# A modulation vector on GpSimd: whole-unit multiply and halving sums, or 512-column products summed one by one

## The chip, the cores and the metric

The kernel runs on one core of a Trainium2 chip. The metric is the device time of one execution in microseconds; the profile gives one execution in detail, on that core. Engines are named as the profile names them: PE (TensorE matmul), PEld (its weight load), DVE (VectorE), ACT (ScalarE), POOL (GpSimd) and SP (the queue that issues the weight loads).

## The reference

Two blocks run one after the other over 256 tokens of width 1024, all in float32. The first is a two-layer mixer (gated recurrence, latent attention, memory attention, each layer ending in a layer norm), the second has attention, pooling and a layer of 16384 experts. The part that the change touches is the modulation of the second block, which depends on `c` alone and on nothing that the first block computes:

```python
mod = jnp.einsum('bd,de->be', jax.nn.silu(c), w_ada[l]) + b_ada[l]      # (1, 1024) x (1024, 6144)
sh1, sc1, g1, sh2, sc2, g2 = jnp.split(mod[:, None, :], N_MOD, axis=-1)
h = rmsnorm(x, norm1_g[l]) * (1.0 + sc1) + sh1
```

## The kernel before

The order of all work is written out by hand as a text of tasks, `LAYER` for each of the two layers and `BLOCK2` for the second block; every engine walks the same text and takes its part of each task. The weights arrive in units of 2 MB (1024 rows by 512 columns, laid out as 128 partitions by 8 chunks of 512) in a ring of three slots. The load of unit n is issued by SP when PE has counted unit n - 3 as done.

Twelve of the tasks are called `AD`, six in each layer: each makes 512 of the 6144 numbers of the modulation vector. GpSimd works on the unit where it lies. The chunk index c and the partition p together are the row of the weight, and `silu_c` (a view into tile `lbt`, 128 x 8) holds silu(c) in the same layout, so what is wanted is the sum over c of `w[:, c, :] * silu_c[:, c]`, a 128 x 512 tile called `part` (half of `mod_part`, the two halves in turn), which PE then sums over the partitions with four small matmuls (line 761) and DVE adds to the bias (line 1329). GpSimd does it in four instructions, each of which waits for the one before by `pool_step`: line 510 multiplies all 4096 columns, with `silu_c` broadcast along the 512 columns of a chunk; line 511 adds the upper four chunks to the lower four (2048 columns), line 512 the upper two of these to the lower two (1024 columns), line 513 the last two into `part` (512 columns). PE waits on `mod_partial` before line 761, and counts the unit as done after it.

The places of the `AD` tasks in `LAYER` that the steps below speak of:

- the first of a layer stands in the text after `F1 Da01 Da02 Db01 L00 A0`; but GpSimd starts as soon as its unit has landed, while PE still runs F1 (line 570, 64 matmuls) and DVE the rotations of UP (lines 1440, 1442 and 1443). DVE then takes F1 from PSUM (line 1359), does `Da01`, `Da02` and `Db01` (two instructions each: lines 1385 and 1389 twice, then 1396 and 1397), and PE's matmuls of level 1 (line 726) wait for `Db01`.
- the second of a layer runs beside Q1 (PE line 570).
- the fifth and sixth close the layer: `O2 L18 H10 AD H11 AD H12 O3 O1 LN`. H10, H11 and H12 are short matmuls on PE (lines 742 to 744 and 751), O3 and O1 are output products (line 608).

DVE instructions that matter in what follows read two operands from SBUF: line 1350 (`sm` times a broadcast of `stat`), 1385 and 1389 (differences of `b`), 1396 and 1397 (`big` times `kT` or `qT`), 1442 and 1443. Lines 1359, 1411, 1455 and 1476 read one operand from PSUM. The scores of a head, line 622 on PE, are taken from PSUM by line 1455.

After the two layers the second block runs; from about 970 us on, its experts fetch 8 KB rows by indirect DMA, with DVE, ACT and PE behind the DMA.

Of the kernel before, what the change touches and what calls it, by code (L numbers as in the profile page):

```python
# [14 lines left out]
P = 128  # L15
# [3 lines left out]
DC = D_MODEL // P  # L19
# [11 lines left out]
COLS = 512  # L31
# [137 lines left out]
def part_starts():  # L169

    return {tile * PICKS + first * TOPK: n + 1 for n, (tile, first, last) in enumerate(EXPERT_PARTS)}
# [48 lines left out]
def build(nc, d, out):  # L220
# [10 lines left out]
    with ExitStack() as ctx:  # L231
# [58 lines left out]
        silu_c = lbt[:, 4, :]  # L290
# [41 lines left out]
        def sem(name):  # L332
            if name not in made:
                made[name] = ctx.enter_context(nc.semaphore(name))
            return made[name]
# [19 lines left out]
        def bank_filled(eng, key):  # L355
            eng.wait_ge(sem("bank_filled"), BANK[key] + 1)
# [18 lines left out]
        def ring_loads(n):  # L375

            units = range(n % RING, n + 1, RING)
            return 16 * sum(3 if STREAM[k][1] == "UP" else 1 for k in units)

        def unit_done(eng, l, name):  # L380
            eng.wait_ge(sem("unit_done"), UNIT[l, name] + 1)

        def steps(eng, own):


            seen = {}

            def step(ins, name=None, value=None, behind=0):
                name = name or own
                seen[name] = value or seen.get(name, 0) + 1  # L390
                ins.then_inc(sem(name), 1)
                eng.wait_ge(sem(name), seen[name] - behind)
            return step
# [100 lines left out]
        @block.gpsimd  # L494
        def _(pool):
            g = nc.gpsimd
            do = steps(pool, "pool_step")

            pool.wait_ge(sem("silu_c"), 1)
            for l in range(DEPTH + 1):  # L500
                for task in TASKS[l]:
                    if task[:2] == "AD":
                        j, n = int(task[2:]), UNIT[l, task]
                        pool.wait_ge(sem(f"ring_load{n % RING}"), ring_loads(n))
                        if j >= 2:
                            key = (l, (f"AD{j - 2}",)) if (l, (f"AD{j - 2}",)) in BANK else (l - 1, (f"AD{j - 2}",))
                            bank_filled(pool, key)
                        w = ring[:, n % RING, :].rearrange("p (c n) -> p c n", c=DC)
                        part = mod_part[:, j % 2, :]
                        do(g.tensor_tensor(w, w, silu_c.unsqueeze(2).to_broadcast([P, DC, COLS]), ALU.mult))  # L510
                        do(g.tensor_tensor(w[:, 0:4, :], w[:, 0:4, :], w[:, 4:8, :], ALU.add))  # L511
                        do(g.tensor_tensor(w[:, 0:2, :], w[:, 0:2, :], w[:, 2:4, :], ALU.add))
                        do(g.tensor_tensor(part, w[:, 0, :], w[:, 1, :], ALU.add), "mod_partial")

            pool.wait_ge(sem("uT_ready"), 1)
            pool.wait_ge(sem("b2_load"), 16 * N_B2)
            do(g.tensor_copy(pool_sum, uT))
            for w in range(4):
                for k in range(w + 1):
                    n = 2 ** k  # L520
                    spare = mixed[:, w, :]
                    do(g.tensor_copy(spare, pool_sum[:, w, :]))
                    do(g.tensor_tensor(pool_sum[:, w, n:T], spare[:, n:T], spare[:, 0:T - n], ALU.add))
            do(g.tensor_tensor(mixed, pool_sum, inv_count.rearrange("p (a t) -> p a t", a=4), ALU.mult))
            do(g.tensor_tensor(mixed, mixed, uT, ALU.subtract), "pool_mixed")


            starts = part_starts()
            for n in range(ROWS):
                t, j, k = n // PICKS, n % PICKS, n % N_SLOTS  # L530
                if n in starts:
                    pool.wait_ge(sem("experts"), starts[n])
                if n >= N_SLOTS:
                    pool.wait_ge(sem("rows_used"), n - N_SLOTS + 1)
                elif n in freed_with:
                    if freed_with[n][0] == "K":
                        unit_done(pool, B2, freed_with[n])
                    else:
                        bank_filled(pool, (B2, ("E", 7)))
                pool.indirect_dma_start(row_slot[k], None, d["peer_uv_2"],  # L540
                                        bass.IndirectOffsetOnAxis(ap=expert[:, t, j:j + 1], axis=0))\
                    .then_inc(sem(f"row_load{k}"), 16)
# [696 lines left out]
        def _(dve):  # L1239
# [112 lines left out]
            for l in range(DEPTH):  # L1352
                for task in TASKS[l]:
# [25 lines left out]
                    elif task[:2] == "Da":  # L1379
                        g, m = int(task[2]), int(task[3])  # L1380
                        if m >= 3:

                            bank_filled(dve, (l, ("L", g, m - 3, 1)))
                        b0, b1, w0, w1, _, _, mid = level_views(g, m)
                        do(v.tensor_tensor(w0, mid, b0, ALU.subtract))
                        if m == 8:
# [3 lines left out]
                    elif task[:2] == "Db":  # L1390
                        g, m = int(task[2]), int(task[3])
                        after(dve, "lvl_exp", l, 8 * g + m - 1)
                        _, _, w0, w1, k0, q1, _ = level_views(g, m)
                        if m == 1:
                            after(dve, "q_ready", l, g)
# [366 lines left out]
```

## Time and profile before

| | us |
|---|---|
| median of three runs | 1699.2 (1698.88 to 1701.31) |
| the profiled execution, its own time | 1703.25 |
| its span | 1701.4 |
| PE busy | 1433.9 (84%) |
| DVE busy | 895.8 (53%) |
| POOL busy | 451.8 (27%) |
| POOL line 510, 12 instructions | 84.6, mean 7.048 |
| POOL line 511, 12 instructions | 56.7, mean 4.729 |
| POOL line 512, 12 instructions | 29.8, mean 2.487 |
| POOL line 513, 12 instructions | 17.8, mean 1.487 |

The span is the time from the first to the last instruction of the profiled execution; its own time is 1.85 us longer and lies 4.05 us above the median of the three runs. Busy time is a sum over instructions, not a share of what sets the end. The twelve modulation units keep GpSimd busy for 188.9 us together, all of it between 102 and 800 us of the span.

### The profile page before, as it was taken

The numbers are of one execution on the slowest core, as the hardware profiler recorded it, in microseconds if no ns is written. First come the engines' busy times: TensorE is split into PE (matmuls) and PEld (weight loads), VectorE is DVE, ScalarE is ACT, GpSimd is POOL, SyncE is SP. The second block draws the span as 40 slices with busy tenths as digits, with TensorE's granted clock in tenths as the row PEclk, the third lists the DMA queues.
The fourth block names the chain that finished last, engine by engine and source line by source line (L and its number), as shares of the span: only waits on it lengthen the run. The fifth ranks groups of instructions, "written<-read, shape, count | busy, mean of one in ns | idle before, by whom it ended". The sixth has DMA issues, their size and how long they took to land.

```text
span 1701.4 us, 14497 instructions
## 1 busy us (share of the span) xinstructions
PE 1433.9 (84%) x4979; PEld 891.3 (52%) x4979; DVE 895.8 (53%) x1689; ACT 425.0 (25%) x1035; POOL 451.8 (27%) x331
## 2 busy tenths in 40 slices
PE   7989898799998898799797988978767888777875
PEld 6768576565767757574374477423322333333332
DVE  2276834544047944643404257785798555444443
ACT  2322232311142214220212223322223222222222
POOL 0033330042003630007004002534333433333330
PEclk9989898999999889899898899989988999899998
DMA  7323442225342435125522137999999999999993
GB/s 261 130 100 104 148 159 84 99 100 219 124 148 80 168 108 189 50 99 192 177 99 99 50 109 299 422 422 421 422 421 421 421 422 421 422 422 421 421 422 134
DMA packets 97460, 401.06 MB, mean 236 GB/s; under 512 B 5765, under 2 KB 9706, under 8 KB 64618
## 3 DMA queue, kind: packets, MB, share of 16 engines
q0 software_dynamic: 36864, 268.45, 38.1%
q1 hardware_dynamic: 60522, 131.68, 21.7%
q8 instruction: 40, 0.66, 0.2%
q14 instruction: 34, 0.28, 0.0%
HBM read 399.06 MB, written 1.05 MB: 235 GB/s over the span
## 4 chain that ended last, share of the span: by engine, by line
PE 53%; DMA 22%; DVE 11%; issue 6%; ACT 6%; POOL 1%; ACTq 0%; SPq 0%; DVEq 0%; POOLq 0%
PE pj L570 21%; DMA ring<-in_peer_uv,vM 9%; PE bank L927 8%; PE pj L608 7%; PE pj L583 5%; PE bank L726 3%; DMA kM<-in_peer_uv,vM 3%; DMA hv<-in_peer_uv,vM 3%; DMA yT<-in_peer_uv,vM 3%; PE bank L638 2%; DMA more_rows<-in_peer_uv,vM 2%; DMA b<-in_peer_uv,vM 1%; PE bank L552 1%; DMA qM<-in_peer_uv,vM 1%; PE bank L622 1%
## 5 line engine op out<-in xcount | busy, mean ns | idle before, releaser
L570 PE MATMUL pj<-xT,ring 128*128 128x256 f32 (+1 forms) x1664 | 373.8, 387 | 2.3 <-ACTq L976 2.3
L570 PEld LDWEIGHTS pj<-xT,ring 128*128 128x128 f32 (+1 forms) x1664 | 318.8, 193 | 55.1 <-issue 5.8
L510 POOL TENSOR_TENSOR ring<-ring,lbt 128x4096 f32<-128x4096 f32 x12 | 84.6, 7048 | 607.6 <-issue 475.4
L540 POOL DMA_INDIRECT ring<-in_peer_uv,vM x102 | 95.7, 939 | 168.3 <-PE bank L927 139.7
L608 PE MATMUL pj<-ring,yT 128*128 128x512 f32 x320 | 138.9, 593 | 0.9 <-ACTq L1180 0.5
L927 PE MATMUL bank<-ring,far_pair 128*128 128x512 f32 x208 | 103.4, 650 | 31.0 <-ACT far_pair L1215 31.0
L1207 ACT ACTIVATE rope<-vM 128x4 f32<-128x4 f32 x64 | 13.1, 205 | 450.7 <-DVE big L1685 450.6
L927 PE MATMUL bank<-ring,causal 128*128 128x512 f32 x200 | 97.6, 639 | 21.5 <-ACT causal L1215 20.3
L608 PEld LDWEIGHTS pj<-ring,yT 128*128 128x128 f32 x320 | 60.3, 190 | 75.5 <-issue 73.7
L726 PE MATMUL bank<-big 128*128 128x128 f32 x480 | 79.5, 332 | 15.4 <-DVE big L1397 10.4
L927 PEld LDWEIGHTS bank<-ring,far_pair 128*128 128x128 f32 x208 | 42.5, 209 | 91.1 <-issue 51.6
L726 PEld LDWEIGHTS bank<-big 128*128 128x128 f32 x480 | 75.5, 242 | 24.7 <-DVE big L1397 11.2
L1685 DVE SCALAR_TENSOR_TENSOR pair<-ring,pj 128x1024 f32<-128x1024 f32 x51 | 62.2, 1220 | 48.6 <-DMA ring<-in_peer_uv,vM 44.5
L1685 DVE SCALAR_TENSOR_TENSOR big<-ring,pj 128x1024 f32<-128x1024 f32 x51 | 62.2, 1220 | 46.8 <-DMA ring<-in_peer_uv,vM 46.8
L927 PEld LDWEIGHTS bank<-ring,causal 128*128 128x128 f32 x200 | 40.1, 204 | 77.8 <-issue 50.4
L1045 ACT ACTIVATE big<-big 128x1024 f32<-128x1024 f32 x32 | 33.8, 1058 | 128.2 <-DVE big L1389 124.3
L583 PE MATMUL pj<-ring,xT 128*128 128x512 f32 x128 | 57.6, 609 | 0.0
L1411 DVE COPY_PREDICATED pair<-level_mask,bank 128x512 f32<-128x512 uint8 x56 | 40.8, 729 | 30.9 <-PE bank L726 29.3
L511 POOL TENSOR_TENSOR ring<-ring 128x2048 f32<-128x2048 f32 x12 | 56.7, 4729 | 0.9
L982 ACT ACTIVATE sm<-sm,stat 128x256 f32<-128x256 f32 x64 | 32.5, 508 | 94.3 <-DVE stat L1460 69.9
L1209 ACT ACTIVATE rope<-rope,rstd 128x1 f32<-128x1 f32 x256 | 54.4, 282 | 2.1
L540 POOL DMA_INDIRECT more_rows<-in_peer_uv,vM x18 | 18.0, 998 | 117.9 <-DVE vM L1596 86.5
(341 smaller groups left out, 2273.1 us busy)
## 6 DMA issues: line engine op xcount, KB each, us to landing
ring<-in_w_in SPq DMA_DIRECT2D x26, 2048.0 KB, 7.9
ring<-in_w_ada SPq DMA_DIRECT2D x12, 2048.0 KB, 8.0
ring<-in_w_out SPq DMA_DIRECT2D x10, 2048.0 KB, 7.8
ring<-in_peer_wq SPq DMA_DIRECT2D x4, 2048.0 KB, 8.0
ring<-in_w_mem_k SPq DMA_DIRECT2D x2, 2048.0 KB, 11.9
ring<-in_w_mem_v SPq DMA_DIRECT2D x2, 2048.0 KB, 9.3
ring<-in_w_in SPq DMA_DIRECT2D x2, 1664.0 KB, 9.6
ring<-in_peer_uv,vM POOLq DMA_INDIRECT x102, 24.8
```

The source lines that it names most:

```text
L510: do(g.tensor_tensor(w, w, silu_c.unsqueeze(2).to_broadcast([P, DC, COLS]), ALU.mult))
L511: do(g.tensor_tensor(w[:, 0:4, :], w[:, 0:4, :], w[:, 4:8, :], ALU.add))
L540: pool.indirect_dma_start(row_slot[k], None, d["peer_uv_2"], bass.IndirectOffsetOnAxis(ap=expert[:, t, j:j + 1], axis=0))\
L570: ins = nc.tensor.matmul(pj[s][0:n, 2 * m:2 * m + T], w[:, c, m:m + n], act[:, c, :], start=(c == 0), stop=(c == DC - 1))
L583: ins = nc.tensor.matmul(pj[s][:, t * COLS:(t + 1) * COLS], act[:, c, t * P:(t + 1) * P], w[:, c, :], start=(c == 0), stop=(c == DC - 1))
L608: ins = nc.tensor.matmul(pj[t][:, n * 512:(n + 1) * 512], yT[:, 4 * j + c, t * P:(t + 1) * P], w[:, c, n * 512:(n + 1) * 512], start=(firs ...
L638: ins = nc.tensor.matmul(bank_of(key)[rows, 0:T], v[s], pT[:, i % 2, s, :], start=(s == 0), stop=(s == TT - 1))
L726: ins = nc.tensor.matmul(B[:, n * P:(n + 1) * P], k, q, start=True, stop=True)
L927: ins = nc.tensor.matmul(bank[2 * t + half][:, :], diag[n % N_DIAG], row_slot[n % N_SLOTS][:, c0:c0 + COLS], start=(j == 0), stop=(j == PI ...
L1209: a.activation(weights_of[:, n0 + k:n0 + k + 1], acts[:, n0 + k:n0 + k + 1], ACT.Copy, scale=gate[:, t, j + k:j + k + 1]).then_inc(sem("ro ...
L1411: do(v.copy_predicated(dst, level_mask[:, m - 1:m, :].to_broadcast([P, 4, P]), B), *bank_free(key))
L1685: v.scalar_tensor_tensor(out=junk[n % 2], in0=row_slot[k][:, 0:D_MODEL], scalar=1.0, in1=pj[BIG[l, f"K{2 + t}"][0]][:, :], op0=ALU.mult, o ...
```

## The change

On GpSimd the four instructions of a unit become fifteen, all over 512 columns. The first multiplies chunk 0 by a scalar per partition, `silu_c[:, 0:1]`, straight into `part`. Then for each of the seven other chunks one instruction multiplies the chunk in place by its scalar, and one adds it to `part`. Each still waits for the one before. The last addition gives `mod_partial`. Nothing else in the kernel differs.

```diff
-                        do(g.tensor_tensor(w, w, silu_c.unsqueeze(2).to_broadcast([P, DC, COLS]), ALU.mult))
-                        do(g.tensor_tensor(w[:, 0:4, :], w[:, 0:4, :], w[:, 4:8, :], ALU.add))
-                        do(g.tensor_tensor(w[:, 0:2, :], w[:, 0:2, :], w[:, 2:4, :], ALU.add))
-                        do(g.tensor_tensor(part, w[:, 0, :], w[:, 1, :], ALU.add), "mod_partial")
+                        do(g.tensor_scalar(part, w[:, 0, :], silu_c[:, 0:1], None, ALU.mult))
+                        for c in range(1, DC):
+                            do(g.tensor_scalar(w[:, c, :], w[:, c, :], silu_c[:, c:c + 1], None, ALU.mult))
+                            do(g.tensor_tensor(part, part, w[:, c, :], ALU.add), "mod_partial" if c == DC - 1 else None)
```

The order of instructions is the same as before on PE, DVE, ACT and SP. On POOL, at the twelfth unit (the last `AD` of the second layer, after which its next work is the copy of line 517 in the second block), it was:

```order
L510 TENSOR_TENSOR ring<-ring,lbt 128x4096 [waits bank_filled,ring_load2,mod_partial]
L511 TENSOR_TENSOR ring<-ring 128x2048 [waits pool_step]
L512 TENSOR_TENSOR ring<-ring 128x1024 [waits pool_step]
L513 TENSOR_TENSOR mod_part<-ring 128x512 [waits pool_step]
L517 COPY kT<-kT 128x1024 [waits b2_load,uT_ready,mod_partial]
```

The same unit begins now with these rows, of which the second and third come seven times:

```order
L510 TENSOR_SCALAR mod_part<-ring,lbt 128x512 [waits bank_filled,ring_load2,mod_partial]
L512 TENSOR_SCALAR ring<-ring,lbt 128x512 [waits pool_step]
L513 TENSOR_TENSOR mod_part<-mod_part,ring 128x512 [waits pool_step]
L512 TENSOR_SCALAR ring<-ring,lbt 128x512 [waits pool_step]
L513 TENSOR_TENSOR mod_part<-mod_part,ring 128x512 [waits pool_step]
```

Four rows in a chain have become fifteen in a chain, with the same waits at the head; the wait for the unit's bank now stands ahead of the first write to `mod_part`, where it stood before too. On PE the end of the same unit is awaited here, between H11 (line 751) and H12 (the second row of line 751), as before:

```order
L751 MATMUL bank<-sq,ones_mean 128x512 [waits ho_sq,bank_free2]
L761 MATMUL bank<-ones_mean,mod_part 128x1 [waits mod_partial,bank_free3]
L761 MATMUL bank<-ones_mean,mod_part 128x1 x3
L751 MATMUL bank<-sq,ones_mean 128x512 [waits bank_filled,ho_sq,bank_free0]
L608 MATMUL pj<-ring,yT 128x512 [waits ring_load0,y_att]
```

No row of PE has moved; what changes there is only when `mod_partial` comes.

## Rows read from the trace of the kernel before

**Rows 1.** The page: busy time, share of the span and instructions of each engine

```profile
PE 1433.9 (84%) x4979; PEld 891.3 (52%) x4979; DVE 895.8 (53%) x1689; ACT 425.0 (25%) x1035; POOL 451.8 (27%) x331
```

**Rows 2.** Chain that ended last, 764 to 812 us: start, us, what

```profile
775.80 5.67 DMA ring<-in_w_ada
781.47 3.08 issue
784.55 7.03 POOL ring L510
...
791.64 4.52 POOL ring L511
...
796.23 2.35 POOL ring L512
...
798.65 1.27 POOL mod_part L513
...
800.06 1.04 PE bank L761 x8
```

**Rows 3.** Timeline of PE, 384 to 400 us, layer 1: start, us, instruction, idle before

```profile
393.17 1.02 PE L761 MATMUL bank<-ones_mean,mod_part 128*128 128x1 f32 x8 [0.98 <-POOL mod_part L513]
394.50 1.10 PE L751 MATMUL bank<-sq,ones_mean 128*128 128x512 f32 x2 [0.30 <-ACT sq L1104]
```

**Rows 4.** Timeline of POOL, 911 to 915 us: copies with one input

```profile
911.97 1.03 POOL L517 COPY kT<-kT 128x1024 f32<-128x1024 f32 x1 [112.05 <-ACTq L1152]
913.06 0.40 POOL L522 COPY b<-kT 128x256 f32<-128x256 f32 x1
```

**Rows 5.** Waits: who waited for whom, us in total, times, longest

```profile
PE bank L726 <- DVE big L1397: 10.4, 2, 5.6
```

**Rows 6.** Timeline of DVE, 511 to 531 us, first unit of layer 2

```profile
511.63 6.81 DVE L1442 TENSOR_TENSOR qM<-qM,rope 32x512 f32<-32x512 f32 x1
518.47 4.88 DVE L1443 TENSOR_TENSOR qM<-qM,sm 32x512 f32<-32x512 f32 x1
523.39 1.23 DVE L1359 TENSOR_SCALAR b<-pj 128x1024 f32<-128x1024 f32 x1
524.76 1.36 DVE L1385 TENSOR_TENSOR big<-b 128x512 f32<-128x512 f32 x1
526.16 1.63 DVE L1389 TENSOR_TENSOR big<-b 128x512 f32<-128x512 f32 x1
...
530.01 0.69 DVE L1397 TENSOR_TENSOR big<-big,qT 128x512 f32<-128x512 f32 x1
```

**Rows 7.** Timeline of POOL, 510 to 530 us, the same unit

```profile
510.88 7.02 POOL L510 TENSOR_TENSOR ring<-ring,lbt 128x4096 f32<-128x4096 f32 x1 [117.85 <-issue]
517.97 4.84 POOL L511 TENSOR_TENSOR ring<-ring 128x2048 f32<-128x2048 f32 x1
...
525.65 1.59 POOL L513 TENSOR_TENSOR mod_part<-ring 128x512 f32<-128x512 f32 x1
```

**Rows 8.** Timeline of PE, 505 to 535 us, the same stretch

```profile
507.00 15.55 PE L570 MATMUL pj<-xT,ring 128*128 128x256 f32 x64
...
530.76 3.54 PE L726 MATMUL bank<-big 128*128 128x128 f32 x16 [5.56 <-DVE big L1397]
```

**Rows 9.** Timeline of POOL, first unit of layer 1

```profile
102.72 7.24 POOL L510 TENSOR_TENSOR ring<-ring,lbt 128x4096 f32<-128x4096 f32 x1 [102.27 <-DMA ring<-in_w_ada]
```

**Rows 10.** Timeline of DVE, the same unit

```profile
116.49 1.37 DVE L1385 TENSOR_TENSOR big<-b 128x512 f32<-128x512 f32 x1
```

**Rows 11.** Timeline of PE, the same unit

```profile
122.49 2.72 PE L726 MATMUL bank<-big 128*128 128x128 f32 x11 [4.83 <-DVE big L1397]
```

**Rows 12.** Timelines of PE, then of DVE, second unit of layer 2

```profile
574.81 1.03 PE L622 MATMUL bank<-kM,qM 96*128 96x256 f32 x4
...
576.76 0.69 DVE L1455 SCALAR_TENSOR_TENSOR sm<-bank,causal 128x512 f32<-128x512 f32 x1 [0.21 <-DVE pair L1411]
...
557.64 7.28 DVE L1350 TENSOR_TENSOR sm<-sm,stat 128x512 f32<-128x512 f32 x1
```

## The prediction

> **What bounds the kernel now.** I read the page first. PE is busy 84% of the span, DVE 53%, POOL 27% [rows 1], and that 27% counts the expert fetches of the second half too. So GpSimd's throughput binds nothing. Its modulation work can matter in two ways only: PE waits for a unit's result, or DVE, sharing something with it, becomes late while PE waits for DVE. The second view, the chain that ended last, names the one place where the first way holds: the twelfth unit. Its load is issued at 775.80, GpSimd starts at 784.55, and its four instructions lie end to end in the chain until PE's line 761 at 800.06, behind which line 751 and the output products follow without another wait [rows 2]. The sixth unit, the same place one layer earlier, is nearly as tight: PE idles 0.98 us until GpSimd's line 513 ends, starts line 761 at 393.17 and line 751 at 394.50, for which ACT had been ready at about the same time [rows 3]. All other units are finished long before PE wants them.
>
> For the second way I looked at the timelines of DVE and POOL side by side. DVE's line 1442, with two inputs in SBUF, takes 6.81 us at 511.63, where line 1397, of the same kind, takes 0.69 us at 530.01 [rows 6]. Line 510 on POOL runs from 510.88 to 517.90 [rows 7], and the DVE instruction ends at 518.44, 0.54 us behind it. The same holds at 526.16: line 1389 ends at 527.79, 0.55 us behind the end of line 513 (525.65 + 1.59 = 527.24). So a DVE instruction with two SBUF inputs stands still until the POOL instruction under way ends. The price on the other side is small: line 513 takes 1.59 us here and 1.27 us in the chain of the twelfth unit [rows 7, 2], so a POOL instruction that finds DVE inside is 0.33 us longer, once. Is PE late through this? The view of waits has one line that says so: line 726 waits for DVE's line 1397 twice, 10.4 us in all [rows 5]; these are the first units of the two layers [rows 8, 11]. In the other units PE is in a long product while DVE stands still.
>
> **The cost of a unit.** Undisturbed, before: 784.55 to 799.92, so 15.37 us, gaps of 0.07 us between instructions included [rows 2]. After: 7 additions over 512 columns at 1.27 us, the line 513 of the chain, make 8.89; 14 gaps make 0.98; and 8 products by a scalar over 512 columns, of which the trace has none. From below: a copy, one input and one output, takes 1.03 us over 1024 columns and 0.40 over 256 [rows 4], a line that gives 0.61 at 512. From above: line 510, which reads a second operand for each element, if only by broadcast. Take from the additions what an instruction costs beside its elements: 4.52, 2.35 and 1.27 us over 2048, 1024 and 512 columns [rows 2] leave 0.18 us at zero columns; then 7.03 us over 4096 columns is 1.67 ns a column, and 512 of them are 1.03 us. I take 0.80, about the middle, a little nearer the copy: the product reads one stream like the copy, but fetches a scalar and multiplies. The unit is then 6.40 + 8.89 + 0.98 = 16.3 us, **0.9 us more** than before; with the copy's price 14.75 (0.6 less), with the broadcast's 18.1 (2.7 more). What was won by touching less data in wide sums is little, since both forms multiply 4096 columns and add 3584.
>
> By the Trainium skill (GPSIMD Engine Reference, section 3.1) a tight loop on GpSimd took 769 ns for 512 elements, which as a price of the product would make the unit 16.0 us and the sum about 1 us smaller.
>
> **Where it is paid.**
> - Twelfth unit: on the path whole, +0.9. Its start is set by its load (775.80), which waits for an output product and not for GpSimd; the eleventh unit leaves 3.08 us of nothing before it [rows 2] and can end up to 3.1 us later before it holds this one up.
> - Sixth unit: PE waits for it already, and line 751 follows 1.33 us behind the start of line 761 [rows 3], +0.9. A gain here would be worth nothing, since ACT's `sq` released line 751 too.
> - First unit of layer 2. DVE no longer stands still for 6.8 and 4.9 us at 511.63, and can start line 1359 when PE's F1 is in (507.00 + 15.55) instead of at 523.39 [rows 8, 6]: its first line 1385 starts at 523.9, 0.8 us earlier. But GpSimd is not through by then: of its 16.3 us, 12.4 are done (13.0 less two delays of 0.33), 3.9 are left, nearly four pieces of 1.09, and each now meets one DVE instruction, so they last 5.2 us, to 529.1. DVE does one instruction for each, so four, is free at 529.65, does the last two at 0.73 each and ends at 531.1, where before it was 530.70: +0.4.
> - First unit of layer 1, in the same way: GpSimd starts at 102.72, line 1385 on DVE at 116.49 [rows 9, 10]. 13.4 us are done by then, 2.8 left, three pieces, to 120.3 with three delays; DVE is free at 120.85 and ends its last three at 123.0; before, PE's line 726 was released at 122.44 [rows 11]: +0.6.
> - Second unit of layer 2: the scores are in PSUM about 1.58 us behind the start of line 622, at 576.39, the lag that the same pair has in layer 1; DVE took them at 576.76, because contended instructions had made it late [rows 12]. With pieces it is in time: -0.4.
> - The other seven: nothing. DVE stands still inside products of PE's of some 15 us (that of 507.00 is one [rows 8]) and has caught up at their end, since the one line of the waits that has PE behind a contended DVE instruction counts two cases [rows 5]; with pieces it is never later. If that cover were thinner, DVE's relief would be a gain (below), not a loss.
> - PE's, ACT's, DVE's and SP's instructions and all loads stay. The eleven more instructions a unit cost issue time only in the gaps, counted above.
>
> Sum: 0.9 + 0.9 + 0.4 + 0.6 - 0.4 = **+2.4 us**, on an execution of 1703.25 whose span is 1701.4. Its own time lies 4.05 above the median of the runs, 1699.2; put on that median, the change gives **1701.6 us**. It is 0.14%; a measurement of this kernel tells about 0.2%, 3.4 us, from no change.
>
> **The rivals.**
> 1. *The scalar product is as cheap as a copy*, 0.61 us. The unit is 0.6 us shorter: twelfth -0.6, sixth 0, first of layer 2 -0.4 (2.35 us left at 523.9, two pieces), first of layer 1 -0.6, second -0.4: -2.0, or 1697.2. For it: one stream in, one out. Against it: the scalar. Within the 0.2% all the same. The Trainium skill says of this (GPSIMD Engine Reference, section 4.1) that operations with one input run at roughly line rate on GpSimd; the copies agree, and whether a product with a scalar operand does no row shows.
> 2. *The scalar product costs what the broadcast product does*, 1.03 us, and the change ends slower. Place: the sixth and twelfth units, on PE's path. The unit is 2.7 us longer: +5.4 there; first of layer 2 +1.9 (5.7 us left, five pieces), first of layer 1 +2.1, second -0.4: +9.0, or 1708.2. It passes 3.4 us from about 0.84 us a product on. For it: on this engine every element passes through a program, and 15 short instructions pay 15 launches. Against it: half the operands.
> 3. *DVE's relief is worth more than I let it be.* In the first and second units of layer 2, DVE's lines 1442, 1443 and 1350 take 6.81, 4.88 and 7.28 us in place of 0.69 [rows 6, 12], 16.9 us of standing still. If PE truly ran behind DVE there, these would come back, at 1682.3 if nothing is lost elsewhere. Against it: in the same stretch PE's F1 ends at 522.55 only and the next product at about 575, so at most 0.8 and 0.4 us are free [rows 8, 12]. The rule behind it is in the Trainium skill (SBUF — State Buffer, Who interferes with whom): GpSimd and a DVE instruction with two SBUF inputs exclude each other for the whole instruction, so shorter instructions would mean shorter waits. The trace agrees on the wait [rows 6, 7]; it is PE's products that make it nearly worthless.
>
> **How the numbers follow.** The forecast, with the product at 0.68 to 0.88 us, holds 0.45 (sums of -0.5 to +4.7); rival 1 0.25, rival 2 0.25, rival 3 0.05. Slower by over 0.2% is rival 2 and the third of the forecast above 0.84 us: 0.40. Faster by over 0.2% is rival 3 and 0.03 of rival 1, if a measurement adds its own: 0.08. The rest is 0.52. The range takes in rivals 1 and 2 and 0.3 to 0.7 us of scatter at either end: 1696.5 to 1708.5; left out are rival 3 and prices above the broadcast's.
>
> **What would show it.** On POOL, products (lines 510 and 512) with a duration of 0.80 us and additions at 1.27, or 1.6 where DVE meets them; a twelfth unit of 16.3 us from its load to PE's line 761, which then starts about 16.4 us behind it. On DVE no instruction of 512 columns above about 2 us before 800 us, so less busy time by some tens of microseconds. PE's line 726 released by DVE later by about half a microsecond in the first units. The prediction is wrong if the twelfth unit is shorter than before or longer than 17.5 us, or if PE's start of the output products at the end of either layer comes earlier by several microseconds, which would be rival 3.

## The result and the profile after

| | us |
|---|---|
| changed kernel, median of four runs | 1726.23 (1720.21 to 1727.65) |
| kernel before, beside it | 1699.12 (1698.88 to 1701.31) |
| ratio | 1.0136, interval 1.0108 to 1.0165 |
| profiled execution of the changed kernel | 1727.65, its span 1725.9 |

The change makes the kernel slower by 1.4%, outside the range that was given. The medians lie 27.1 us apart, and the span of the profiled execution grew by 24.5 us. The page's first part and the groups of the three changed lines (us busy, mean ns of one, idle before):

```profile
PE 1439.8 (83%) x4979; PEld 893.8 (52%) x4979; DVE 832.1 (48%) x1689; ACT 424.9 (25%) x1035; POOL 529.2 (31%) x463
...
L510 POOL TENSOR_SCALAR mod_part<-ring,lbt 128x512 f32<-128x512 f32 x12 | 18.8, 1567 | 540.4 <-issue 417.0
...
L512 POOL TENSOR_SCALAR ring<-ring,lbt 128x512 f32<-128x512 f32 x84 | 138.6, 1650 | 8.2
...
L513 POOL TENSOR_TENSOR mod_part<-mod_part,ring 128x512 f32<-128x512 f32 x84 | 109.1, 1299 | 7.0
```

DVE is busy 63.7 us less than in [rows 1]. POOL is busy 77.4 us more, and the cause stands in the first two groups: a product by a scalar takes 1.56 us or more, where the forecast had 0.80. The additions cost what was expected. POOL's timeline through the end of layer 2 shows the price of one unit and what it does to the next:

```profile
776.80 1.61 POOL L510 TENSOR_SCALAR mod_part<-ring,lbt 128x512 f32<-128x512 f32 x1 [116.12 <-issue]
778.50 1.56 POOL L512 TENSOR_SCALAR ring<-ring,lbt 128x512 f32<-128x512 f32 x1
780.14 1.26 POOL L513 TENSOR_TENSOR mod_part<-mod_part,ring 128x512 f32<-128x512 f32 x1
...
798.22 1.26 POOL L513 TENSOR_TENSOR mod_part<-mod_part,ring 128x512 f32<-128x512 f32 x1
799.58 1.56 POOL L510 TENSOR_SCALAR mod_part<-ring,lbt 128x512 f32<-128x512 f32 x1
...
816.28 1.88 POOL L512 TENSOR_SCALAR ring<-ring,lbt 128x512 f32<-128x512 f32 x1
...
821.25 1.26 POOL L513 TENSOR_TENSOR mod_part<-mod_part,ring 128x512 f32<-128x512 f32 x1
```

The eleventh unit runs from 776.80 to 799.48, 22.7 us instead of 15.4. It passes the 3.08 us of nothing that lay ahead of the twelfth [rows 2], so the twelfth starts on its heels, at 799.58, and takes 22.9 us itself. PE meets both delays at once. Its timeline at the end of layer 1 and of layer 2 in the changed kernel, then at the end of layer 2 in the kernel before:

```profile
385.89 0.95 PE L761 MATMUL bank<-ones_mean,mod_part 128*128 128x1 f32 x8
...
388.56 1.02 PE L751 MATMUL bank<-sq,ones_mean 128*128 128x512 f32 x2
402.98 1.83 PE L761 MATMUL bank<-ones_mean,mod_part 128*128 128x1 f32 x8 [13.40 <-POOL mod_part L513]
405.12 2.04 PE L751 MATMUL bank<-sq,ones_mean 128*128 128x512 f32 x2 [0.30 <-PE bank L761]
...
822.66 1.83 PE L761 MATMUL bank<-ones_mean,mod_part 128*128 128x1 f32 x8 [13.41 <-POOL mod_part L513]
824.79 2.05 PE L751 MATMUL bank<-sq,ones_mean 128*128 128x512 f32 x2 [0.30 <-PE bank L761]
```

```profile
800.06 1.02 PE L761 MATMUL bank<-ones_mean,mod_part 128*128 128x1 f32 x8 [1.89 <-POOL mod_part L513]
801.39 1.10 PE L751 MATMUL bank<-sq,ones_mean 128*128 128x512 f32 x2 [0.30 <-PE bank L761]
```

And its line in the waits (us in total, times, longest), now and before:

```profile
PE bank L761 <- POOL mod_part L513: 26.8, 2, 13.4
```

```profile
PE bank L761 <- POOL mod_part L513: 2.9, 2, 1.9
```

PE waits 23.9 us more for GpSimd. It also comes back slower: lines 761 and 751 take 1.83 and 2.04 us where they took 1.02 and 1.10 [rows 3]. The stretches show the granted clock there; first the changed kernel, then the one before (us, busy time of PE, PEld, DVE, ACT and POOL with instructions, granted clock, DMA share, GB/s):

```profile
385.00:400.00 15.00, 4.28 (x32) 3.40 (x30) 6.03 (x9) 2.51 (x4) 14.09 (x11) 0.83 0.86 332
400.00:410.00 10.00, 6.72 (x16) 4.01 (x17) 1.43 (x3) 1.32 (x2) 2.75 (x2) 0.58 0.34 114
```

```profile
400.00:410.00 10.00, 10.00 (x24) 4.37 (x23) 4.18 (x6) 0.91 (x2) 0.00 (x0) 1.00 0.61 229
```

After 13.4 us in which PE did nothing the mean grant over ten microseconds is 0.58, near the lower of the two levels (1.2 of 2.4 GHz), where before it was 1.00. That costs 1.75 us on lines 761 and 751 at the end of each layer, and 0.75 and 0.83 us on the 64 output products behind them (27.63 us before, 28.38 and 28.46 now).

In time order the 24.5 us are: -2.6 up to the fifth unit's line 761 (388.50 before, 385.89 now), +13.7 from there to the eleventh unit's (405.98 to 419.66 us long), +13.4 from there to the end. Longer waits and late return together make 29.0 us, more than the whole. The -2.6 is within the scatter: four executions further down whose early units are wide reach that line between 384.11 and 388.96 us. Another 1.9 us come back in PE's other work behind it, of which 1.3 lie in a stretch of layer 2 where the grant was 0.93 instead of 0.92.

DVE's long standing still is gone, as expected, and hardly matters for the time. In the first unit of layer 1, DVE, then POOL and PE:

```profile
102.56 0.81 DVE L1442 TENSOR_TENSOR qM<-qM,rope 32x512 f32<-32x512 f32 x1
103.41 0.68 DVE L1443 TENSOR_TENSOR qM<-qM,sm 32x512 f32<-32x512 f32 x1
...
116.49 1.06 DVE L1389 TENSOR_TENSOR big<-b 128x512 f32<-128x512 f32 x1
117.58 0.69 DVE L1385 TENSOR_TENSOR big<-b 128x512 f32<-128x512 f32 x1
118.31 1.64 DVE L1389 TENSOR_TENSOR big<-b 128x512 f32<-128x512 f32 x1
```

```profile
116.00 1.88 POOL L512 TENSOR_SCALAR ring<-ring,lbt 128x512 f32<-128x512 f32 x1
117.97 1.43 POOL L513 TENSOR_TENSOR mod_part<-mod_part,ring 128x512 f32<-128x512 f32 x1
```

```profile
121.83 3.62 PE L726 MATMUL bank<-big 128*128 128x128 f32 x16 [5.65 <-DVE big L1397]
```

No DVE instruction on two SBUF inputs lasts over 1.7 us there, yet PE waits for it 5.65 us where it waited 4.83 [rows 11].

These rows also show that the two forms on POOL don't hold DVE up alike. The DVE instruction at 118.31 ends at 119.95, 0.55 us behind the addition that it met (117.97 + 1.43). The one at 116.49 ends at 117.55, 0.33 us before the product by a scalar that it met (116.00 + 1.88), and has lost only 0.37 us. In the whole changed kernel it is the same: of DVE's lines 1385, 1389, 1396 and 1397, the fourteen that began beside an addition ended 0.54 to 0.56 us behind it, and the twelve that began in the first 0.7 us of a product by a scalar ended 0.33 to 0.34 us before its end.

### The profile page after: what moved, and what is told of

The parts are those of the page before. It is cut to its first block, busy times and chain, and to the rows that moved or that the text cites. A ratio compares the mean times of both kernels' runs of the same rounds, so it can differ in the third digit from the quotient of the medians.

```text
span 1725.9 us, 14629 instructions
## 1 busy us (share of the span) xinstructions
PE 1439.8 (83%) x4979; PEld 893.8 (52%) x4979; DVE 832.1 (48%) x1689; ACT 424.9 (25%) x1035; POOL 529.2 (31%) x463
## 4 chain that ended last, share of the span: by engine, by line
PE 30%; DMA 22%; issue 11%; DVE 7%; ACT 3%; POOL 3%; ACTq 0%; DVEq 0%; POOLq 0%
PE pj L570 10%; DMA ring<-in_peer_uv,vM 8%; PE bank L927 7%; PE pj L608 5%; DMA yT<-in_peer_uv,vM 4%; DMA kM<-in_peer_uv,vM 3%; DMA hv<-in_peer_uv,vM 3%; PE pj L583 2%; DMA b<-in_peer_uv,vM 1%; DMA qvE<-in_peer_uv,vM 1%; POOL ring L512 1%; DMA qM<-in_peer_uv,vM 1%; POOL mod_part L513 1%; PE pj L676 1%; PE bank L726 1%
## 5 line engine op out<-in xcount | busy, mean ns | idle before, releaser
L570 PE MATMUL pj<-xT,ring 128*128 128x256 f32 (+1 forms) x1664 | 369.9, 384 | 2.3 <-ACTq L976 2.3
L510 POOL TENSOR_SCALAR mod_part<-ring,lbt 128x512 f32<-128x512 f32 x12 | 18.8, 1567 | 540.4 <-issue 417.0
L512 POOL TENSOR_SCALAR ring<-ring,lbt 128x512 f32<-128x512 f32 x84 | 138.6, 1650 | 8.2
L513 POOL TENSOR_TENSOR mod_part<-mod_part,ring 128x512 f32<-128x512 f32 x84 | 109.1, 1299 | 7.0
L726 PE MATMUL bank<-big 128*128 128x128 f32 x480 | 79.8, 332 | 16.3 <-DVE big L1397 11.2
L1455 DVE SCALAR_TENSOR_TENSOR sm<-bank,causal 128x512 f32<-128x512 f32 x16 | 11.1, 692 | 102.7 <-PE bank L552 80.6
```

What stands on the lines that cost most here:

```text
L510: do(g.tensor_scalar(part, w[:, 0, :], silu_c[:, 0:1], None, ALU.mult))
L512: do(g.tensor_scalar(w[:, c, :], w[:, c, :], silu_c[:, c:c + 1], None, ALU.mult))
L513: do(g.tensor_tensor(part, part, w[:, c, :], ALU.add), "mod_partial" if c == DC - 1 else None)
L570: ins = nc.tensor.matmul(pj[s][0:n, 2 * m:2 * m + T], w[:, c, m:m + n], act[:, c, :], start=(c == 0), stop=(c == DC - 1))
L726: ins = nc.tensor.matmul(B[:, n * P:(n + 1) * P], k, q, start=True, stop=True)
```

## The experiments

Three questions were put. Does the loss lie in the two units that close each layer, and there alone? What in the product makes it dear? And is DVE's relief worth something where nothing hides it? In kernels that hold both forms, all lines behind 510 stand six higher. The kernel before, measured beside each, has run medians of 1699 to 1706 us. Its granted clock over an execution lies between 0.911 and 0.927, and its span goes with it by about -0.84 us for each 0.001 (94 executions, correlation -0.65); differences of a few microseconds are read from stretches of the trace for that reason.

**The old form in the last two units of each layer**

```diff
+if j % 6 < 4:      # pieces, as in the change
+else:              # the four wide instructions
```

> The last two units of each layer in the old four instructions, the first four in the fifteen pieces. Theory A (the product by a scalar costs 1.56 us, and this is paid only where PE waits for the last unit of a layer): PE's wait before line 761 falls from 13.4 us back to about 1 to 2 in both layers, and the time is that of before or 1 to 3 us below it, 1696 to 1699. Rival B (the pieces cost time everywhere, by taking turns with DVE eight times more often): four of six units still pay, about two thirds of the 25 us, 1712 to 1716.

Measured: 1700.01 us (1695.86 to 1706.84), ratio 0.9985 [0.9963, 1.0008]. PE waits 2.5 us for GpSimd. With eight of twelve units in the new form nothing measurable is lost or won.

**The new form in the last two units alone**

```diff
+if j % 6 >= 4:     # pieces; else wide
```

> The reverse: only the last two units of each layer in pieces. Theory A: the whole loss is here, PE's waits of about 13 us are back, 1723 to 1728. Rival B: a third of the loss, 1705 to 1709.

Measured: 1723.3 us (1720.79 to 1726.44), ratio 1.0125 [1.0081, 1.0169], wait 26.8 us. Repeated:

> The kernel with the last two units of each layer in scalar pieces, once more. As it ran the first time: about 20 us above before.

1724.83 us, 1.0144 [1.0102, 1.0185], wait 26.8 again. Four units of twelve carry the loss.

**The new form in the very last unit of each layer**

```diff
+if j % 6 == 5:     # pieces; else wide
```

> Only the last unit of each layer in pieces, so that the fifth ends early and does not hold up the sixth. Theory A: the unit is 22.6 us in place of 15.4, PE waits 7.2 us longer twice, so 14.5 us, and up to 3 more if PE comes back at a lower clock: 1713 to 1717. If instead the whole loss came from the last unit alone, it would stay at 1724 or more. Rival B: a sixth of the loss, 1703.

> The kernel with only the last unit of each layer in scalar pieces, once more. If the first result was a matter of the clock, it now lies 14 to 19 us above before and below the run with the last two units, with granted clocks alike in the two. If a long wait costs more than its length, it again lies at 23 and not below the other.

The wait did what was expected: 17.3 us (8.55 and 8.73), 9.5 less than with both units, which is the part that the fifth and eleventh hand on. The time did not: 1726.2 us, 1.0142 [1.01, 1.0184], and in the repetition 1726.58, 1.0145 [1.0107, 1.0182], where at most 1717 was expected. Here are three stretches that run the same program, from layer 2's first product on `xT` (line 576) to the second unit's line 767: this kernel twice, then the one with both units new.

```profile
450.31:596.40 146.09, 133.75 (x580) 106.41 (x580) 81.37 (x90) 36.02 (x52) 34.67 (x9) 0.90 0.34 119
```

```profile
452.20:598.12 145.92, 133.75 (x581) 106.38 (x581) 80.96 (x90) 36.03 (x52) 34.28 (x9) 0.90 0.34 119
```

```profile
451.44:593.25 141.81, 128.11 (x581) 103.45 (x581) 80.63 (x89) 36.10 (x52) 33.44 (x9) 0.93 0.35 122
```

The last kernel's repetition has 141.73 us at 0.93. The same instructions take 4.2 us longer at a grant of 0.90, with PE 5.6 us busier. From the last line 767 to the first expert fetch, 748 PE instructions in each, it is 220.84 and 220.98 us at 0.89 against 216.87 and 216.40 at 0.91; from that fetch to the end all four lie between 683.8 and 684.4. So about 8 us of the gap goes with the clock and not with the wait for GpSimd. Up to the fifth unit's line 767 another 2.9 us lie between the two kernels on average, although PE waits for GpSimd in neither. Whether the grant follows from how layer 1 ended, and how, is open; the kernel before lies between, 143.48 us at 0.92.

**Products with a broadcast scalar, in pieces**

```diff
-g.tensor_scalar(w[:, c, :], w[:, c, :], silu_c[:, c:c + 1], None, ALU.mult)
+g.tensor_tensor(w[:, c, :], w[:, c, :], silu_c[:, c:c + 1].to_broadcast([P, COLS]), ALU.mult)
```

> The same fifteen pieces, but each product as a product of two tensors with the scalar broadcast along 512 columns, as in the old line 510. Theory A (it is the scalar form that is dear): 1.03 us a piece in place of 1.56, a unit of 18.1 us, the fifth no longer holds up the sixth, +2.7 us a layer: 1702 to 1706. Rival C (any short instruction is dear, by its launch): the pieces stay near 1.5 us, and the time near 1724.

Measured: 1712.94 us (1709.83 to 1715.19), ratio 1.0068 [1.0048, 1.0088]; wait 9.8 us.

```profile
L512 POOL TENSOR_TENSOR ring<-ring,lbt 128x512 f32<-128x512 f32 x84 | 93.5, 1114 | 6.6
...
L510 POOL TENSOR_TENSOR mod_part<-ring,lbt 128x512 f32<-128x512 f32 x12 | 12.8, 1069 | 573.0 <-issue 444.5 <-DMA ring<-in_w_ada 128.0 <-POOL mod_part L513 0.5
```

The form that reads a second operand for every element costs 1.07 us, the one that holds a scalar 1.57. This one edit gives back half of the loss. It was expected at 1702 to 1706 and missed by 7 us. Two things were not in that sum. The wait of 4.71 us at the end of layer 1 already makes lines 761 and 751 come back at 1.41 and 2.04 us. And in the first units PE waits for DVE 13.9 us in all, where it waited 10.4 before and 11.2 with scalar products: beside a broadcast product DVE stands still to 0.55 us behind its end, as beside an addition.

**The scalar products, then the old wide sums**

```diff
+for c in range(DC): g.tensor_scalar(w[:, c, :], ..., ALU.mult)
+# then the three wide additions of the kernel before
```

> Eight products by a scalar over 512 columns in place of line 510, then the old wide additions. Theory A: 8 x 1.56 + gaps + 8.1 = 21.3 us a unit, 5.9 more than before; the fifth unit ends after the load of the sixth and holds it up by 2 to 3 us; PE waits 8 to 9 us longer in each layer: 1715 to 1720. If the short additions and their gaps were the loss instead, the time would be that of before, 1699 to 1702.

Measured: 1737.93 us (1733.4 to 1740.0), ratio 1.0214 [1.0174, 1.0253], the slowest of all and 14 us or more above what was expected, though the wait for GpSimd is 22.3 us, less than the change's. The rest is elsewhere:

```profile
PE bank L762 <- POOL mod_part L514: 22.3, 2, 11.2
PE bank L727 <- DVE big L1398: 20.6, 2, 10.4
```

The lines stand one higher here: the second is line 726's wait of the first units, 11.2 us in the changed kernel. The wide sums, pushed back by slow products, now lie where DVE has its two-input work and PE waits for it. Line 552 waits longer for DVE's line 1350 too, 12.0 us against 7.8. So the piecewise sums of the change do help against this, by 9 us at line 726 alone.

**Prices, by a probe**

```diff
+for _ in range(3): # per unit one form: scalar product over 128 << j columns,
+                   # constant, broadcast, copy, product of two tensors
```

> Prices by themselves. This kernel leaves the modulation product out and multiplies by the wrong numbers instead: in each unit one form of instruction three times, then the old additions. Units 1 to 6: product by a scalar per partition over 128, 256, 512, 1024, 2048 and 4096 columns; unit 7: by a constant over 512; units 8 to 10: broadcast product over 512, 1024 and 2048; unit 11: copy over 512; unit 12: product of two tensors over 512. Theory A1 (dear per element): 512 columns 1.56 us, 4096 about 11 us. Theory A2 (dear per instruction, by fetching the scalar): 0.9 us fixed, 128 columns about 1.0 us, 4096 about 5 to 6 us; then the constant is about 0.6 us at 512. The broadcast product is expected at 1.03 us over 512 columns, the copy at 0.61, the product of two tensors at 1.27.

POOL's timeline, three of a form drawn together, their gaps (0.08 us) inside:

```profile
211.76 8.71 POOL L514 TENSOR_SCALAR ring<-ring,lbt 128x1024 f32<-128x1024 f32 x3 [24.49 <-issue]
...
352.42 16.69 POOL L514 TENSOR_SCALAR ring<-ring,lbt 128x2048 f32<-128x2048 f32 x3 [123.22 <-issue]
...
377.54 32.03 POOL L514 TENSOR_SCALAR ring<-ring,lbt 128x4096 f32<-128x4096 f32 x3
...
537.34 4.79 POOL L516 TENSOR_SCALAR ring<-ring 128x512 f32<-128x512 f32 x3 [119.44 <-issue]
...
652.32 10.96 POOL L519 TENSOR_TENSOR ring<-ring,lbt 128x2048 f32<-128x2048 f32 x3 [27.89 <-issue]
...
810.79 3.95 POOL L523 TENSOR_TENSOR ring<-ring 128x512 f32<-128x512 f32 x3 [7.44 <-issue]
```

Less the gaps, a scalar product takes 2.85, 5.51 and 10.62 us over 1024, 2048 and 4096 columns: 2.5 ns a column, and some 0.3 us beside. It is no cheaper with a constant in the instruction (1.54 us over 512), so fetching the scalar isn't what costs. The broadcast product takes 3.60 us over 2048 columns and a product of two tensors 1.26 over 512; a copy took 0.78 here, where sixteen of the copies' run below have 0.613. The form of the instruction is dear, per element, at each of these sizes.

**No product and one sum per unit**

```diff
+g.tensor_tensor(part, w[:, 0, :], w[:, 1, :], ALU.add)   # all that is left
```

> Leaves out the modulation product and two of the three additions: a unit is one addition of 512 columns, 1.27 us. It shows what all of GpSimd's work on the units costs the kernel before. Theory A: PE's two waits of 1.0 and 1.9 us and one to three us of DVE lateness, so 1693 to 1697. Rival D (DVE's standing still is on the path, 17 us or more): 1682 or less.

Measured: 1694.42 us (1690.13 to 1700.97), ratio 0.9963 [0.9941, 0.9986]. All that GpSimd's modulation work cost the kernel before, but for one addition a unit, is some 6 us (2 to 10 by the interval), DVE's standing still included. A relief worth 17 us, the third rival, is excluded.

**Eight idle copies ahead of the last unit, in the kernel before**

```diff
+for _ in range(8 if j % 6 == 5 else 0): g.tensor_copy(part, w[:, 0, :])
```

> The kernel before, with eight copies of 512 columns put ahead of the last unit of each layer, whose results are overwritten. At 0.83 us each with its gap they lengthen that unit by 6.6 us, about as much as the pieces did when only the last unit had them, and touch nothing else. Theory A with PE coming back slowly: 2 x 6.6 and 2 x 2.5 for the clock, 16 to 19 us above before. If it is 22 or more, as with the pieces in the last unit alone, then a long wait costs PE more than its length and its first products; if 13, the pieces cost something of their own.

Measured: 1712.52 us (1709.98 to 1717.79), ratio 1.0074 [1.0048, 1.0101]. A copy of 512 columns takes 0.613 us (sixteen, by the lines view), the very value that the forecast had drawn for it. PE's wait grows by 10.0 us to 12.9, and the medians lie 10.6 us apart (12.6 by the ratio), so lateness alone, with no arithmetic behind it and the old form throughout, costs what PE waits and a little more. The 16 to 19 that the text expected was too much: it had each wait 6.6 us longer, and each was 5.0.

**The last two units moved to where PE has other work**

Both `AD` out of the tail, to behind `L12` and `L15`: in the form of the change, in the old form, in broadcast pieces.

```diff
-H02 Da14 Db13 L12 A11 ... L15 A14 ... L18 H10 AD H11 AD H12
+H02 Da14 Db13 L12 AD A11 ... L15 AD A14 ... L18 H10 H11 H12
```

> The fifteen pieces of the change kept as they are, but the last two AD tasks of each layer moved forward in the text, behind L12 and L15, where GpSimd has been idle for 100 us, so that PE asks for each unit long after it is done. Theory A (the loss is only PE waiting for the last unit of a layer): the whole loss of some 25 us goes, PE's wait on GpSimd is 0, and the time is that of before less its own waits of 1.0 and 1.9 us, so 1 to 6 us below before. Rival B (the pieces cost through DVE or in the many instructions): at least 8 us of the loss stay.

> The old four instructions with the same move. Theory A: 1 to 4 us below before, the two waits of 2.9 us together. Against the run with the pieces moved it shows what the pieces are worth to DVE where their price is covered: theory A says the pieces are then 0 to 4 us better, rival B that they are worse.

> The same move with the fifteen pieces whose products are broadcast products of 1.1 us. Theory A: as fast as or up to 2 us faster than with the scalar products, since the unit is shorter and meets DVE less often, 2 to 6 us below before.

Measured: 1.0038 [1.0021, 1.0055], 1.0077 [1.0053, 1.01] and 1.0021 [1.0002, 1.004] (1707.77, 1714.53 and 1705.65 us). The change's own instructions, in another place, lose some 6 us instead of 27: none of PE's wait for GpSimd is left. But all three had been expected below the kernel before, and none is: something in this place costs more than the 2.9 us of waiting that it saves, and only part of it was found. The wide form is the worst of the three:

```profile
PE bank L622 <- DVE yT L1486: 12.8, 2, 6.5
```

```profile
PE bank L622 <- DVE yT L1486: 23.1, 2, 12.1
```

The first line is the change's form, the second the wide one; the kernel before has 9.7. Where PE truly waits for DVE, pieces win, here by 7 us.

**Only one of the two moved, behind `L15`**

```diff
-L15 A14 ... L18 H10 AD H11 AD H12
+L15 AD A14 ... L18 H10 AD H11 H12
```

> The old four instructions, one tail unit of each layer moved forward behind L15. Theory A: PE's two waits of 1.0 and 1.9 us go, 0 to 3 us below before; if the moved unit stops DVE where PE waits for it, up to 5 us above.

> All units in pieces with broadcast products, and one of the two tail units of each layer moved forward behind L15, so that the other finds GpSimd idle and starts about 15 us earlier. Theory A: PE's wait for GpSimd is 0 (it was 9.8 us with these pieces and 2.9 before), 2 to 6 us below before. If the moved unit meets DVE where PE waits for DVE, up to 4 us of that go again.

> The fifteen scalar pieces of the change, one tail unit of each layer moved forward behind L15. Theory A: the other tail unit starts about 15 us earlier, 22.6 us of work fit before PE asks, PE's wait is 0 to 1 us, and the loss of 25 us is gone: within 4 us of before. Rival B (pieces cost elsewhere): 8 us or more above.

Wide: 1725.75 us, 1.013 [1.0102, 1.0158]. Broadcast pieces: 1707.96, 1.0043 [1.0019, 1.0067]. Scalar pieces: 1709.79, 1.0033 [1.0018, 1.0048]. PE doesn't wait for GpSimd in any of them, but the wide one was expected at most 5 us above the kernel before and is 20 us above by the medians, and the broadcast pieces, expected below it, are 6 above. The scalar pieces are 4 above, at the edge of what was expected. The wide one's POOL and DVE side by side:

```profile
298.47 7.01 POOL L510 TENSOR_TENSOR ring<-ring,lbt 128x4096 f32<-128x4096 f32 x1 [73.26 <-issue]
305.56 4.82 POOL L511 TENSOR_TENSOR ring<-ring 128x2048 f32<-128x2048 f32 x1
```

```profile
301.24 4.79 DVE L1495 TENSOR_TENSOR yT<-yT,rstd 128x512 f32<-128x512 f32 x1
306.06 4.87 DVE L1385 TENSOR_TENSOR big<-b 128x512 f32<-128x512 f32 x1
```

DVE ends 0.55 us behind each POOL instruction, as in [rows 6, 7], but nothing hides it here: PE's idle time before line 638 is 37.6 us in all, against 21.7 with broadcast pieces, 19.7 with scalar pieces and 14.3 before. In this place the change's form, with its dear product, beats the old one by 16 us. The waits differ by 18.

**The early units in broadcast pieces, the last two wide**

```diff
+if j % 6 < 4:      # broadcast pieces; else wide
```

> The first four units of each layer in fifteen pieces with broadcast products (1.07 us each), the last two in the old four instructions. Theory A: nobody waits longer for GpSimd, DVE stands still less: 0 to 4 us below before. If DVE's relief were nothing, the same time as before.

Measured: 1700.23 us (1695.97 to 1703.43), ratio 0.9988 [0.9964, 1.0012]. The best of both forms in the old places is no better than the kernel before within what can be told. PE's wait for DVE in the first units is 15.3 us here against 10.4, so the broadcast pieces lose there what they may win elsewhere. No version that computes the whole vector was measurably faster than the kernel before.

## Why the prediction was wrong, step by step

- **"The cost of a unit", the product by a scalar: this step failed.** The price of 0.80 us was 1.56. Its upper bound, 1.03, came from the broadcast product, with the reason that this one reads a second operand for each element. Broadcast pieces then measured 1.07, so the number was right and the reasoning was not: a form that moves less data isn't therefore cheaper on GpSimd. The bound from above should have been left open, since no row had the form. The unit is 22.7 us, 7.3 more, not 0.9.
- **"Where it is paid", the twelfth unit: right in kind, too small.** Its start was said to hang on its load as long as the eleventh ends less than 3.1 us later. It ended 7.3 later. The start slipped by 7.3 - 3.1 = 4.2 us, and with its own 7.6 (22.93 less 15.37) that makes 11.8; PE's wait grew by 11.5. The threshold had been named but never priced, since at 0.80 us it wasn't reached.
- **The sixth unit: the same.** That the fifth could hold it up was not considered. It too starts on the heels of the one before, at 379.92, 0.11 us behind the end of the fifth. Before, that gap was 2.19 us (375.47 to 377.66), so the same working gives 7.3 - 2.2 + 7.6 = 12.7; the wait grew by 12.4. For both layers the prediction's own working with 1.56 us put in gives 24.5 us of waiting, and 23.9 were measured.
- **PE's return at a lower clock: missing.** The sum took a wait as its length. Lines 761 and 751 then cost 1.8 us more per layer, in the copies run too, and the output products 0.8 more. The trace of the kernel before had the sign of it: at 555.07, behind a wait of 3.00 us for DVE, line 761 takes 1.87 us. That the measured 24.5 is so near the waits alone is chance, as the account in time order shows.
- **The second rival, slower by the sixth and twelfth unit,** had the place and the mechanism of what came. It was priced at 1708.2 with 1.03 us, and by its own words it decides from 0.84 us on. Broadcast pieces were measured 1.0068 times the kernel before, 11.5 us above it where the rival had 9.0; of its parts, 5.4 at the two last units was 6.9 us of wait, and 4.0 in the first units was 3.5.
- **First units: near in number, by luck.** Predicted +0.6 in layer 1 and +0.4 in layer 2, read as PE's wait for line 1397: +0.8 (5.65 against 4.83) and about nothing (11.2 - 5.65 against 5.56). But the working had DVE stand to the end of every piece that it meets. With the real unit of 22.7 us, 9.3 are left at 116.49, six pieces of 1.5 and one DVE instruction to each, and that working gives some 5 us in each layer (an estimate from these numbers). Two errors offset each other: the product is dearer than thought, and DVE is let go before it ends. With broadcast products, beside which DVE does stand to the end, the two waits grew by 3.5.
- **Second unit of layer 2, -0.4: right where it was looked for, and lost again behind.** DVE takes the scores in time, and line 622 waits 0.56 us where it waited 0.94. But the next line 638 then waits 2.07 us instead of 1.67, and from the first unit's line 761 to the second's it is 29.47 us, and was 29.33. In layer 1 the same line 638 waits 2.07 instead of 1.68 with nothing won before it. These 0.4 us were not in the sum; what line 638 waits for the profile doesn't name.
- **DVE's standing still: right beside additions and broadcast products, wrong beside products by a scalar**, where it is let go 0.33 us before the end. The 0.33 us that a POOL instruction pays: right, 1.88 against 1.56 us at 816.28. The early units are worth nothing measurable (0.9985 and 0.9988). The third rival falls with the run without products. That its mechanism is real where PE waits for DVE is shown by the moved units.
- **The other seven units, nothing: right within what can be told,** by the run with only the tail in the old form, but for the fifth and eleventh, which hand on what they are late.

By the Trainium skill (GPSIMD Engine Reference, section 4.1) operations with one input run at roughly line rate on GpSimd. The copies fit that, 0.613 us over 512 columns where DVE's undisturbed instructions of that size take 0.69; the product by a scalar, one input too, does not: 1.56 us. The measurement decides, and the first rival, which leaned on this rule beside the copies' rows, was off by 29 us.

## What to carry to other kernels

Before an instruction form goes onto a path that another engine waits for, time that form on that engine at that size: a price drawn from other forms is no bound, however plausible the bytes are. When a unit gets longer, count how much of its room each neighbour has, and what the sum becomes once the room is used up, because two delays in a row add at the next wait. And splitting GpSimd's work so that DVE stands still for less time pays only where PE waits for DVE at that moment: 16 us in one place here, 7 in another, and nothing measurable in the kernel's own places.

## What was not expected of the hardware

- On GpSimd a product with a scalar per partition costs 1.56 us over 512 columns in float32 and 2.5 ns for each column more, and with a constant it costs the same over 512 (1.54); a broadcast product takes 1.07 over 512 and 3.60 over 2048, a copy 0.613 over 512.
- That dear product is mild on its neighbour. A DVE instruction with two SBUF inputs that begins beside it ends 0.33 us before it; beside an addition or a broadcast product it ends 0.55 us behind.
- After a PE wait of 4.7 us line 751 takes 2.04 us instead of 1.10; after the 0.98 and 1.89 us of the kernel before it takes 1.10.
- The same PE instructions of one stretch (580 or 581 in the trace) took 141.8 us at a grant of 0.93 and 146.0 at 0.90, each twice, though the two kernels do the same from there on until the eleventh unit. What sets the grant stays open.
